# Two merge products of each decode sample moved ahead of its probability turn in the cache stage of a hybrid decoder step

## What is computed

```
s = einsum('bqhd,bkhd->bhqk', q, k) * HEAD_DIM ** -0.5
s = s + c_q - c_k;  s = where(pos_k <= pos_q, s, NEG_INF)
pr = softmax(s, axis=-1)
ob = einsum('bhqk,bkhd->bqhd', pr, v)
merged = sigmoid(ga) * (oa @ proj_a) + sigmoid(gb) * (ob @ proj_b)
h = h + merged @ w_out
h = h + hier_moe(rms_norm(h, ln2_w))
```

## Time and profile before

| what | us |
|---|---|
| median of three runs (lowest, highest) | 887.76 (885.87, 892.13) |
| span of the profiled execution, first to last instruction | 889.2 |
| PE busy / weight loads / DVE / ACT / POOL | 771.0 / 454.7 / 378.6 / 187.0 / 151.4 |
| mean granted TensorE clock, share of full speed | 0.925 |
| moved by DMA | 220.26 MB, mean 248 GB/s |

### The profile page before, as it was taken

One profiled execution on the slowest core, in us unless ns is written; L12 is line 12 of the kernel. 1 busy time (PEld: TensorE's weight loads), 2 busy tenths in 40 slices (PEclk: granted clock), 3 DMA queues, 4 the chain that ended last, 5 costly groups with the idle time before them and its releaser, 6 DMA issues. The chain is left out here.

```text
span 889.2 us, 20760 instructions
## 1 busy us (share of the span) xinstructions
PE 771.0 (87%) x8681; PEld 454.7 (51%) x8681; DVE 378.6 (43%) x710; ACT 187.0 (21%) x429; POOL 151.4 (17%) x306
## 2 busy tenths in 40 slices
PE   5999899989778979956899887989889997799985
PEld 2445466666566646743566555545454434444411
DVE  3130533239842235466846675723462222422213
ACT  2102122116331111022322321222111110111102
POOL 8400030007040020003323333232000000000000
PEclk9999899998978969968999998989979998999997
DMA  9623141212320212429899999986949999999992
GB/s 320 270 94 119 48 158 48 74 71 85 111 58 20 82 41 45 101 85 362 346 404 368 418 362 419 394 323 221 404 178 428 420 426 421 426 419 426 421 417 77
DMA packets 53047, 220.26 MB, mean 248 GB/s; under 512 B 21871, under 2 KB 23962, under 8 KB 28634
## 3 DMA queue, kind: packets, MB, share of 16 engines
q1 hardware_dynamic: 44976, 183.28, 52.8%
q0 software_dynamic: 7328, 35.48, 10.3%
q10 hardware_dynamic: 650, 0.18, 0.1%
HBM read 211.82 MB, written 7.09 MB: 246 GB/s over the span
## 5 line engine op out<-in xcount | busy, mean ns | idle before, releaser
L230 PE MATMUL bank<-arena 128*128 128x320 f32 x256 | 85.6, 480 | 5.4 <-PEq L112 3.6
L208 POOL DMA_DIRECT2D arena<-in_cv x116 | 59.9, 516 | 112.4 <-PE bank L1831 74.7
L546 PE MATMUL bank<-arena 128*128 128x336 f32 x224 | 71.1, 473 | 4.2 <-DVE arena L712 4.2
L2618 DVE TENSOR_TENSOR arena<-arena,bank 128x512 f32<-128x512 f32 x40 | 27.5, 688 | 109.7 <-PE bank L2399 106.7
L2429 PE MATMUL bank<-arena 128*32 128x512 f32 x512 | 64.6, 607 | 3.7 <-DMA arena<-in_w_exp 2.5
L1524 DVE STREAM_TRANSPOSE arena<-arena 128x2048 f32<-128x2048 f32 x28 | 63.1, 2288 | 5.5 <-DMA arena<-in_ck 4.4
L511 PE MATMUL bank<-arena 128*128 128x512 f32 (+1 forms) x144 | 64.6, 607 | 0.7 <-ACT arena L416 0.7
L230 PEld LDWEIGHTS bank<-arena 128*128 128x128 f32 x256 | 50.2, 207 | 27.3 <-issue 9.9
L546 PEld LDWEIGHTS bank<-arena 128*128 128x128 f32 x224 | 43.8, 200 | 27.3 <-issue 10.0
L1340 ACT ACTIVATE arena<-bank 128x384 f32<-128x384 f32 (+6 forms) x63 | 26.0, 443 | 123.7 <-PE bank L230 46.2
L1831 PE MATMUL bank<-arena 128*16 128x128 f32 x1024 | 35.0, 299 | 17.5 <-issue 9.3
(11 more groups left out here) (491 smaller groups left out, 1115.4 us busy)
## 6 DMA issues: line engine op xcount, KB each, us to landing
arena<-in_w_exp SPq DMA_DIRECT2D x99, 1024.0 KB, 20.2
arena<-in_ck SPq DMA_DIRECT2D x120, 256.0 KB, 6.9
arena<-in_cv POOLq DMA_DIRECT2D x116, 256.0 KB, 9.0
arena<-in_w_gate SPq DMA_DIRECT2D x8, 1024.0 KB, 4.8
arena<-in_w_za SPq DMA_DIRECT2D x7, 1024.0 KB, 6.9
arena<-in_w_zb SPq DMA_DIRECT2D x6, 1024.0 KB, 14.5
arena<-in_w_proj SPq DMA_DIRECT2D x8, 512.0 KB, 10.9
arena<-in_w_out SPq DMA_DIRECT2D x4, 1024.0 KB, 10.8
```

The lines of the kernel that those rows point to most:

```text
L208: eng.dma_start(tile[n:P:4, :], src[bass.ds(page, 1)].rearrange("a (p j) n -> (a p) (j n)", j=4))\
L230: mm = nc.tensor.matmul(bank[b][:, 0:TM], w[:, k, a, :], xnT[:, k, NMETA:T], start=(k == 0), stop=(k == KT - 1))
L546: mm = nc.tensor.matmul(bank[j % 2][:, 0:T], w[:, k, (j % 2) * P:(j % 2 + 1) * P], xnT[:, k, :], start=(k == 0), stop=(k == KT - 1))
```

## The change

A second table, `ahead_no`, splits the fills of a sample in two. For the samples 1, 3, 4, 5 and 6 the first two of the fills that PE did after weigh(b) are done between turn_out(b-1) and turn_probs(b). (For sample 2 and for the last one none is moved.) So fills 5, 6 (kind a), 11, 12 and 14, 15 (kind b), 18, 19 and 24, 25 (kind o) move. `turn_probs(b)` now waits for them to be out of their banks. DVE takes them out directly behind the maxima of sample b+1, ahead of turn_bias, keep_out and turn_keys. No computation is added or removed.

```diff
         fill_no = [0, 0, 5, 8, 11, 14, 18, 24, 28, len(kinds)]
+        ahead_no = [fill_no[n] + (2 if 2 <= n < DB and n != 3 else 0) for n in range(DB + 1)]
...
                     if b:
-                        pe.wait_ge(S("fill_sb"), fill_no[b + 1])
+                        pe.wait_ge(S("fill_sb"), ahead_no[b + 1])
...
+                def fills_ahead(n):
+
+                    for f in range(fill_no[n], ahead_no[n]):
+                        fill(f)
+
                 def fills(n):
 
-                    for f in range(fill_no[n], fill_no[n + 1]):
+                    for f in range(ahead_no[n], fill_no[n + 1]):
                         fill(f)
...
                     if b:
                         turn_out(b - 1)
+                    fills_ahead(b + 1)
                     turn_probs(b)
...
+                def fills_ahead_out(n):
+
+                    for f in range(fill_no[n], ahead_no[n]):
+                        fill_out(f)
+
                 def fills_out(n):
 
-                    for f in range(fill_no[n], fill_no[n + 1]):
+                    for f in range(ahead_no[n], fill_no[n + 1]):
                         fill_out(f)
...
                     nc.vector.tensor_scalar(nm, nm, -1.0, None, mult).then_inc(S("nm_ready"), 1)
+                    fills_ahead_out(b)
                     if b < DB - 1:
                         turn_bias(b + 1)
```

## The result

The changed kernel takes 893.75 us (median of 20 runs, 887.87 to 900.14); the kernel before, timed beside it, 887.95 us (20 runs, 880.34 to 893.42). The ratio is 1.0067, 95% interval 1.0044 to 1.0090: slower by 5.8 us. The forecast was 885.5 in a range of 881 to 890.5, so it had the wrong sign and the time lies above the range. It is within 1%, where 0.93 of the chance stood. The profiled execution spans 892.5 us, 3.3 more than that of before. That is less than the timed 5.8, because the profile of the kernel before shows an execution that was longer than most. In every run on record the time is 1.6 to 1.7 us more than the span of the same execution. So the profiled execution of before took about 890.8 us (an estimate, 889.2 + 1.6), 2.9 above its median and not 1.4; that of the changed kernel took 894.09 us, 0.3 above its median.

The account below looks back on a forecast made before the run. PE's chain in the cache stage was taken to set when the byte-bound expert stream starts. Terms 2.7 - 2.2 + 0.9 + 0.8 = 2.2 us off the 887.76 median gave 885.5 us, range 881 to 890.5.

Parts of the forecast that it names:

- term for the values' pages: Value pages of sample 2: last page 1.1 us later, PE's wait 2.40 becomes 4.6, a loss of 2.2 us.
- Nothing else moves: Rest of the cache stage: later key transposes and exponentials stay covered, so no further cost.
- +1.1 on PE: Sample 1: weighing 3.36 us later with 4.48 us of fills done ahead of it, a gain of 1.1 us.
- the clock: PE's granted clock: work in the gaps may keep it up, +0.8 us, half of sample 1's excess.
- The move at sample 6: PE at sample 6: weighing 3.8 us later for 3.52 us of moved fills, a loss of 0.25 us.
- Samples 3 to 5: PE gains of 0.36 us at sample 3, 0.36 and 1.24 at sample 4, and -0.1 at sample 5.
- What bounds it, and the gap's cause: Cache stage: PE's chain sets when the expert stream starts; the 1.97 us gap before weighing ends with keep_out on DVE.
- The new waits ahead of the turn: PE before each moved turn, waiting for DVE's take-out: 0.7 us at kind a, 0.6 to 1.5 us overall.
- the fourth rival: DVE takes out late, so PE's wait moves ahead of the turn; about 889 us, chance 0.05.
- The 1.24 ahead of fill 16: Sample 4: PE's 1.24 us wait for the additions of fills 14 and 15 disappears, a gain of 1.24.
- The wait for values at sample 4: PE's wait of 1.83 us there becomes anything from 0 to 2.2, taken as 0.9, a gain of 0.9.
- Rival 2: Sample 2's last value page lands the full 3.36 us later and the clock falls: 4.5 slower, 892 us, chance 0.10.

Follow-up runs that it names:

- copy early: Changed kernel, but POOL copies the samples' gates (gs_keep) ahead of its last sixteen value-page issues instead of behind them: ratio 1.0019 to the kernel before.
- keys held back: Changed kernel, SP issuing sample 5's keys only after sample 2's last value pages land: 1.0027 with gates copied before POOL's last page issues, 1.0059 with them copied behind.

## Why the prediction was wrong

Two steps failed, and each costs about the same. The term for the values' pages, -2.2 us, was mis-sized, and "Nothing else moves" put POOL's queue at nothing. Timed alone, the move at sample 1 costs 4.9 thousandths, 4.4 us, where the forecast's own terms (+1.1 on PE, -2.2 for the pages, +0.8 for the clock) make a loss of 0.3. The move at sample 6, with the copy left behind the page issues, costs 4.4 thousandths, 3.9 us, where the forecast had 0.25. Samples 3 to 5 gain 2.4 thousandths, 2.1 us. Together that is 6.9 thousandths, and 6.7 were measured; with intervals of 3 thousandths on each, so close a match is luck.

- *What bounds it, and the gap's cause:* right. The gaps between turn and weighing, 1.97 (samples 1, 3, 4), 0.63 and 1.37 us, all became 0.16 where fills were moved, and 1.97 stayed at sample 2, ending 0.16 behind keep_out there as before. That shows keep_out as the cause of the gap.
- *The new waits ahead of the turn:* right for kinds a and b, forecast 0.7 and 1.4, measured 0.68, 1.39 and 1.39. For kind o the prediction has two numbers: its working (turn at 5.25, fills over at 3.8) makes 1.4, the fourth rival says 0.9. Measured were 1.09 at sample 6 and 0.88 at sample 5, where PE had come 1.39 us late to turn_out, so that the agreement with 0.9 is luck. The 1.24 ahead of fill 16 went.
- *The values' pages:* the mechanism was right, the size is the first step that failed. I took the last page 1.1 us later and the wait as 4.6; it was 2.96 later (499.21 for 496.25) and the waits 5.83. POOL's first issue came 3.30 later (473.16 for 469.86), and from there to the last group it took 26.1 us, before 26.4: only 0.3 us of the shift were made up, where I had assumed that the free bandwidth between 472 and 476 makes up two thirds of it. The wait for values at sample 4, taken as 0.9, measured 2.22. The fourth of these groups also ran slower, 1.91 us for 1.60, and the third 1.91. So scores(4) start 3.3 us later than before (507.86 for 504.54), where the forecast's terms make it 0.3 later. Rival 2 had named a slip of the full 3.36 and 892 us, which is the nearest to the result. But it is only half the cause: the changed kernel with the copy early still has these pages late and stands at 1.0019. The rule of the Trainium skill (DMA: Bandwidth & Descriptors, Queues, rings and completion order), that engines alternate between the queues with work, pointed to this. The trace agrees in that the pages took about 4 us less with the keys held back.
- *"Nothing else moves":* the second step that failed. It looked at keys and exponentials on DVE and ACT, and at POOL only for the values' pages. That their issues are what POOL's next instruction stands behind was left out, though the prediction had worked out that the weighing of sample 6 comes 3.8 us later. Before, the copy was done at 605.74 and PE had ended its turn at 610.26, a slack of 4.5 us. POOL's sixteen issues now start at 597.80 instead of 591.39, 6.4 us later, and PE comes 2.8 us earlier: 6.4 + 2.8 - 4.5 is 4.7, the wait that is there. Price in the profile: 4.9 us of wait and 1.4 of slow fills behind it (8.46 for 7.03). Timed, the four pairs with sample 6 moved that differ only in the copy's place lie 4.8, 7.4, 7.2 and 3.2 thousandths apart (changed kernel, without sample 1, only sample 6, keys held back), 3 to 7 us; the first two pairs were not timed side by side; the medians of the last two are 4.9 and 4.1 us apart. The fifth pair, the kernel before, shows no cost.
- *Sample 6:* forecast a loss of 0.25; with the copy early the move gained (0.9972). The prediction's term leaves out a stall of 2.74 us inside the weighing of sample 6 in the kernel before, and its slow fills stood only in the clock's range. This is tied to the step above. From turn_out(5) to the end of the turn of sample 7 PE took 24.73 us before and 19.06 in the changed kernel, 5.7 less; the weighing of sample 6 came 3.6 later in that stretch, and 3.56 + 5.67 - 4.52 is again 4.7. With the prediction's own numbers (3.8 later, PE no faster) the slack of 4.5 would have covered the shift. Listing POOL's queue alone would therefore not have shown the wait. In this pair of profiles the unforeseen gain and the unforeseen wait nearly cancel: from scores(7) to the last weighing the change costs 0.7 us (38.9 for 38.2), against the forecast's 0.25. The change ends 3.5 us behind in these profiles where the forecast has it 2.2 ahead; of these 5.8 us, 3.0 arise up to scores(4), 2.3 from there to scores(7), and 0.45 behind it.
- *The clock:* forecast +0.8 us; at sample 1 the excess of 1.67 went almost whole (3.96 for 5.36). But the excess is not there in every execution: of the eight profiles that keep the gap at sample 1, four take 5.26 to 5.45 us for this weighing and four 3.69 to 3.78, and the six without the gap 3.69 to 3.96. Half of the excess was thus about right as a mean, for a reason that the prediction did not have. It was given back behind the new waits, as the groups of 1.91 us show.
- *Samples 3 to 5:* forecast 1.9 us with the shorter wait for values left out, measured 0.9976, 2.1 us, with an interval that holds zero. The stall of PE ahead of sample 5's turn_out, for which I had allowed, fell there again (1.39 us).

## What to carry to other kernels

When work is put ahead of a step that releases another engine's queue, list everything that stands behind the released instructions on that queue, and not only the transfers themselves: here one copy of 0.62 us, ready long before, cost 4 to 5 us because it stood behind sixteen DMA issues. The slack of such an instruction must be worked out against how early its user can come, not only against how early it came in one profile. Where two streams fill the DMA, count the slip of a single-buffered one in full: here 3.30 us at the issue were 2.96 at the last page, and holding the other stream back moved the wait to the next sample. When an edit touches several places alike, time the places alone. Here two of five carried the loss: one was better left out, the other became a gain once the copy was moved, and both together gave the fastest version (0.9936 and 0.9954).

## What the runs showed of the hardware

PE stalls for 0.2 to 2.7 us with no releaser ("issue") in the middle of runs of small products, at places that move with the order of the program. For the stall that ended at 596.41 in the kernel before, a 0.3 us window from 593.9 us shows one packet of the instruction queue:

```profile
q8 instruction: 1, 0.02, 20.0%
```

It falls within the wait, 2.4 us before its end. The same holds throughout: between 450 and 625 us the fourteen profiles hold 58 such stalls of 0.23 us or more (the gaps that end with keep_out not counted), and each ends 2.18 to 2.58 us after a packet of that queue (q8) starts. The 37 gaps that end with keep_out show no such tie, 0.8 to 7.3 us. So what PE waits for arrives with that packet. That it is PE's next instructions is an inference from the queue's name; no run here slowed or hastened the fetch alone. In the changed kernel the stall at the place of 596.41 is absent: PE came there later, after two fills and a wait, which would have given the fetch more time. If that is so, moving larger products between runs of small ones can hide such stalls, which the sum of busy times can't tell. In the changed kernel they sat elsewhere too (0.99 us at 546.30, 0.50 at 574.28), so part of what vanished at one place came up at another:

```profile
546.30 1.06 PE L1832 MATMUL bank<-arena 128*16 128x128 f32 x30 [0.99 <-issue]
...
574.28 1.06 PE L1832 MATMUL bank<-arena 128*16 128x128 f32 x30 [0.50 <-issue]
```

The granted clock can differ by a factor of two after waits of different length: windows of the changed kernel (PE, PEld, DVE, ACT, POOL busy, granted clock, DMA share, GB/s) for the weighing of sample 1 after 0.16 us of idling, and for a quarter of the weighing of sample 2 after 3.74:

```profile
471.40:475.70 4.30, 4.27 (x137) 3.58 (x137) 3.10 (x4) 3.09 (x11) 2.08 (x4) 1.00 0.80 267
...
499.20:501.00 1.80, 1.79 (x32) 1.17 (x32) 0.00 (x0) 0.00 (x0) 0.96 (x2) 0.50 0.99 414
```

Full speed (2.4 GHz) in the one, half (1.2 GHz) in the other. So a wait can be paid again in the work behind it, but not each is. A group of four pages takes 1.07 us at full speed and 1.91 at half. It took 1.91 after the waits of 3.74 (changed kernel), 3.89 (without sample 6) and 4.40 us (copy early), but 1.07 after one of 2.22 in the changed kernel, and after a wait of 2.35 it took 1.91 in one kernel (only sample 1) and 1.07 in another (without sample 6).
